# Two-layer hybrid encoder on one core: value blocks by half, keys by part over all partitions, and a new spread of gate pieces

## What is computed

```
h    = RMSNorm(x)
proj = h @ w_in[l]                      # q, k, v and gate columns of three mixers
ya   = windowed attention A  (+-128 tokens, sink, bias)
yb   = dense attention B     (rotary positions)
yc   = dilated attention C   (three patterns: (128,1), (512,4), (2048,16), merged by their denominators)
x    = x + concat[ya*silu(gA), yb*silu(gB), yc*silu(gC)] @ w_out[l]
```

## Time and profile before

| | |
|---|---|
| median of three runs | 2765.29 us |
| the profiled execution | 2772.11 us, of which the span is 2769.8 us |
| TensorE busy | 2732.1 us, 99% of the span |
| VectorE, ScalarE, GpSimd busy | 58%, 43%, 28% |
| mean granted TensorE clock | 0.994 of full |
| layer 0: quads, unit 4, unit 5 | 651.04 to 706.29, to 755.70, to 806.98 us |
| layer 1: quads, unit 4 | 2021.79 to 2082.67, to 2133.26 us |

### The profile page before, as it was taken

One profiled execution on the slowest core, in us unless ns is written; L12 is line 12 of the kernel. 1 busy time (PEld: TensorE's weight loads), 2 busy tenths in 40 slices (PEclk: granted clock), 3 DMA queues, 4 the chain that ended last, 5 costly groups with the idle time before them and its releaser, 6 DMA issues. The chain is left out here.

```text
span 2769.8 us, 43315 instructions
## 1 busy us (share of the span) xinstructions
PE 2732.1 (99%) x14505; PEld 2447.6 (88%) x14505; DVE 1609.7 (58%) x3865; ACT 1184.4 (43%) x2813; POOL 763.8 (28%) x882
## 2 busy tenths in 40 slices
PE   8999999999999999999999999999999999999999
PEld 7888899988999999988888888999889999999887
DVE  3345644434676677677743465444346767776776
ACT  4322222224565566544542222222246655665443
POOL 0333333320343344300003334333203433443000
PEclk9999999999999999999999999999999999999999
DMA  5356566668544542464524565656774445325535
GB/s 175 106 183 200 180 185 188 181 179 233 142 132 123 128 112 82 177 219 130 197 85 142 176 195 173 200 170 188 191 218 134 117 118 149 101 69 217 192 122 182
DMA packets 436214, 442.52 MB, mean 160 GB/s; under 512 B 97591, under 2 KB 327127, under 8 KB 435996
## 3 DMA queue, kind: packets, MB, share of 16 engines
q1 hardware_dynamic: 435996, 439.77, 53.3%
HBM read 313.91 MB, written 125.75 MB: 159 GB/s over the span
## 5 line engine op out<-in xcount | busy, mean ns | idle before, releaser
L1834 ACT CAST w_hi<-w_raw 128x512 fp32r<-128x512 f32 x640 | 397.0, 622 | 697.8 <-PE bank L1605 430.6
L1603 PE MATMUL bank<-w_hi,act_hi 128*128 128x512 f32 x1728 | 689.2, 399 | 0.0
L2120 DVE TENSOR_TENSOR w_lo<-w_raw,w_hi 128x512 fp32r<-128x512 f32 x640 | 460.1, 722 | 384.9 <-ACT w_hi L1834 383.3
L1605 PE MATMUL bank<-w_hi,act_lo 128*128 128x512 f32 x1728 | 679.0, 393 | 0.0
L1604 PE MATMUL bank<-w_lo,act_hi 128*128 128x512 f32 x1728 | 677.6, 392 | 0.0
L1605 PEld LDWEIGHTS bank<-w_hi,act_lo 128*128 128x128 f32 x1728 | 372.6, 216 | 54.1
L1603 PEld LDWEIGHTS bank<-w_hi,act_hi 128*128 128x128 f32 x1728 | 373.3, 216 | 50.1
L1604 PEld LDWEIGHTS bank<-w_lo,act_hi 128*128 128x128 f32 x1728 | 373.3, 216 | 48.7
L1659 PE MATMUL bank<-act_hi,w_hi 128*128 128x384 f32 x1024 | 349.2, 341 | 0.0
L1661 PE MATMUL bank<-act_hi,w_lo 128*128 128x384 f32 x1024 | 346.3, 338 | 0.0
L1660 PE MATMUL bank<-act_lo,w_hi 128*128 128x384 f32 x1024 | 345.7, 338 | 0.0
(11 more groups left out here) (136 smaller groups left out, 4406.5 us busy)
## 6 DMA issues: line engine op xcount, KB each, us to landing
w_raw<-w_in SPq DMA_DIRECT2D x144, 512.0 KB, 4.8
w_sums<-sum_out SPq DMA_DIRECT2D x32, 1280.0 KB, 6.7
w_raw<-w_sums SPq DMA_DIRECT2D x80, 512.0 KB, 4.0
sum_in<-w_out SPq DMA_DIRECT2D x64, 512.0 KB, 5.6
heads_t<-turned SPq DMA_DIRECT2D x240, 128.0 KB, 2.4
q_t<-heads_t SPq DMA_DIRECT2D x192, 128.0 KB, 2.1
k_t<-keys_t SPq DMA_DIRECT2D x48, 384.0 KB, 5.8
w_raw<-w_out SPq DMA_DIRECT2D x32, 512.0 KB, 3.7
```

The source lines that it names most:

```text
L1603: pe.matmul(acc[t][:], hi, w_hi[:, W_AT[n]:W_AT[n] + SLAB], start=(k == 0), stop=False)
L1605: last = pe.matmul(acc[t][:], lo, w_hi[:, W_AT[n]:W_AT[n] + SLAB], start=False, stop=(k == KC - 1))
L1834: nc.scalar.copy(w_hi[:, W_AT[n]:W_AT[n] + SLAB], w_raw[:, load % W_RAW, j, :]).then_inc(w_hi_done, 1)
L2120: nc.vector.tensor_tensor(w_lo[:, W_AT[n]:W_AT[n] + SLAB], w_raw[:, load % W_RAW, j, :], w_hi[:, W_AT[n]:W_AT[n] + SLAB].bitcast(F32), ALU ...
```

## The change

Three edits, and nothing that is computed changes.

1. `load_blocks` takes the half as an argument. The blocks of unit 3 are loaded by half: tiles 0 to 2 at items 17 to 20 (they wait for the value products of unit 1's first three steps alone), tiles 3 to 5 at items 20 to 23. Each half has its own semaphore, and a value product waits for its own half.
2. `load_keys` makes its two DMAs by part: each writes one part (high or low) to all 128 partitions, reading 64 rows of 3072 bytes twice. The bytes are the same.
3. `piece_schedule` has new costs: open quads 3 (were 1), packed quads 4 (were 3), steps of unit 4 6 (were 8), all others 8. By the table that this gives, turns 0 to 23 have 25 pieces (were 14), unit 4 has 44 (was 58), units 5, 8 and 11 have one more each. The splits of gate chunks 4 to 7 move from turns 9, 15, 22 and 25 to 5, 9, 12 and 16; the drain of the first tile's second half from turn 25 to 16, that of the second tile's first half from 32 to 28; the fifth gate load on SP (512 KB) from item 20 to 14, the sixth from 29 to 21.

```
--- before.py
+++ after.py
@@ -565,7 +565,8 @@
 
 def piece_schedule():
 
-    cost = [3 if packed(st["unit"]) else {"Q": 1}.get(st["kind"], 8) for st in STEPS]
+    first_pairs = min(st["u"] for st in STEPS if st["kind"] != "Q")
+    cost = [4 if packed(st["unit"]) else 3 if st["kind"] == "Q" else 6 if st["u"] == first_pairs else 8 for st in STEPS]
     done, now, between = [], 0, PIECES - PIECES_FIRST - PIECES_LAST
     for i in range(N_LOOP):
         if i < N_STEPS:
@@ -634,8 +635,8 @@
 PARTS_AT = at_items((i, x["step"] + MIX_LAG) for i, x in enumerate(ITEMS) if x["kind"] == "Q")
 KEYS_AT = at_items((u, UNIT_LAST[u - KV_SLOTS] + 1) for u in range(KV_SLOTS, len(ATT_UNITS)))
 VALUES_IN_AT = at_items((u, UNIT_LAST[u - KV_SLOTS] + PAIR_LAG + 1) for u in range(KV_SLOTS, len(ATT_UNITS)) if not packed(ATT_UNITS[u]))
-BLOCKS_AT = at_items(((u, c), UNIT_LAST[u - KV_SLOTS] + PAIR_LAG + c)
-                     for u, x in enumerate(ATT_UNITS) if packed(x) and u >= KV_SLOTS for c in range(CLASSES))
+BLOCKS_AT = at_items(((u, half, c), UNIT_START[u - KV_SLOTS] + (half + 1) * (TT // 2) - 1 + PAIR_LAG + c)
+                     for u, x in enumerate(ATT_UNITS) if packed(x) and u >= KV_SLOTS for half in range(2) for c in range(CLASSES))
 MERGE_IN_AT = at_items((mc, end - 2 * TT + 1 + PAIR_LAG + 1 if mc == 0 else MERGE_END[mc - 1] + OWN_TURN + 2) for mc, end in enumerate(MERGE_END))
 BIASES_AT = at_items(((b, heads), BIAS_LAST[b - 2] + 1 + (1 + heads[0] if BIAS_SETS[b][1] is None else 0))
                      for b in range(2, len(BIAS_SETS)) for heads in (((0,), (1,), (2,), (3,)) if BIAS_SETS[b][1] is None else ((0, 1),)))
@@ -904,7 +905,7 @@
         packed_chain = sem("packed_chain")
         blocks_cleared = sem("blocks_cleared")
         ones_set = sem("ones_set")
-        blocks_loaded = sem("blocks_loaded")
+        blocks_loaded = [sem(f"blocks_loaded{i}") for i in range(2)]
         merge_mins = sem("merge_mins")
         merge_args = sem("merge_args")
         merge_exps = sem("merge_exps")
@@ -1241,8 +1242,9 @@
                     sp.wait_ge(scored, l * N_STEPS + UNIT_LAST[u - KV_SLOTS] + 1)
                 elif l > 0:
                     sp.wait_ge(scored, l * N_STEPS)
-                for to in range(2):
-                    sp.dma_start(k_t[to * DH:(to + 1) * DH, :, slot, :, :].bitcast(F32), keys_t[unit["k"]])                        .then_inc(k_loaded[slot], 16)
+                for part in range(2):
+                    rows = bass.AP(keys_t.tensor, (unit["k"] * DH * 2 + part) * TOKENS, [[0, 2], [2 * TOKENS, DH], [1, TOKENS]])
+                    sp.dma_start(k_t[:, part, slot, :, :].rearrange("p t c -> p (t c)").bitcast(F32), rows).then_inc(k_loaded[slot], 16)
 
             def load_values(l, u):
 
@@ -1266,16 +1268,15 @@
                                  v_rows[rows, unit["v"] * DH:(unit["v"] + 1) * DH].rearrange("(t p) n -> p t n", p=P))\
                         .then_inc(shifted_loaded[unit["j"]], 16)
 
-            def load_blocks(l, u, c):
+            def load_blocks(l, u, half, c):
 
                 unit = ATT_UNITS[u]
                 sp.wait_ge(ones_set, 2 * CLASSES * (l + 1))
                 if u >= KV_SLOTS:
-                    sp.wait_ge(pv_done, l * N_STEPS + UNIT_LAST[u - KV_SLOTS] + 1)
+                    sp.wait_ge(pv_done, l * N_STEPS + UNIT_START[u - KV_SLOTS] + (half + 1) * (TT // 2))
                 sp.wait_ge(v_stored, 16 * (l * V_STORES + V_BEFORE_LAST))
                 rows = v_rows[:, unit["v"] * DH:(unit["v"] + 1) * DH].rearrange("(h t m c) n -> h c m t n", h=2, t=TT // 2, c=CLASSES)
-                for half in range(2):
-                    sp.dma_start(blocks[half][c * PACK:(c + 1) * PACK, :, c, 0:DH], rows[half, c]).then_inc(blocks_loaded, 16)
+                sp.dma_start(blocks[half][c * PACK:(c + 1) * PACK, :, c, 0:DH], rows[half, c]).then_inc(blocks_loaded[half], 16)
 
             def load_bias(l, b, heads=range(4)):
                 u, hp = BIAS_SETS[b]
@@ -1470,8 +1471,8 @@
                         load_values(l, 0)
                     if slot == KEYS_SLOT + 1:
                         load_keys(l, 1)
-                        for c in range(CLASSES):
-                            load_blocks(l, 1, c)
+                        for half, c in itertools.product(range(2), range(CLASSES)):
+                            load_blocks(l, 1, half, c)
 
                 for t in range(TT):
                     store_values(l, NS_IN - 1, t)
@@ -1484,8 +1485,8 @@
                         load_keys(l, u)
                     for u in VALUES_IN_AT.get(it, ()):
                         load_values(l, u)
-                    for u, c in BLOCKS_AT.get(it, ()):
-                        load_blocks(l, u, c)
+                    for u, half, c in BLOCKS_AT.get(it, ()):
+                        load_blocks(l, u, half, c)
                     for b, heads in BIASES_AT.get(it, ()):
                         load_bias(l, b, heads)
                     for mc in MERGE_IN_AT.get(it, ()):
@@ -1726,8 +1727,8 @@
                         quad_taken(pe, l, q - 2)
                 pe.wait_ge(ones_set, 2 * CLASSES * (l + 1))
                 if packed(st["unit"]):
-                    pe.wait_ge(blocks_loaded, 16 * 2 * CLASSES * (l * KV_C + st["unit"]["j"] + 1))
                     half, at = divmod(st["t"], TT // 2)
+                    pe.wait_ge(blocks_loaded[half], 16 * CLASSES * (l * KV_C + st["unit"]["j"] + 1))
                     pe.matmul(o[:, 0:CLASSES * (DH + 1)], prob_t[:, n % PT_SLOTS, 0:P],
                               blocks[half][:, at, :, :].rearrange("p c d -> p (c d)"), start=True, stop=True).then_inc(pv_done, 1)
                     return
```

2 lines of the change are left out of this document (1 added, 1 removed).

## The result

| | before | changed |
|---|---|---|
| median | 2765.0 us | 2919.8 us (2919.4 to 2923.5) |
| ratio | 1 | 1.0559 (1.0544 to 1.0574) |
| span of the profiled execution | 2769.8 us | 2917.3 us |

The forecast was 2747 us, its range 2738 to 2758. The time lies far outside. The profile after is read in the same order as that of before.

The account below looks back on a forecast made before the run. TensorE, busy for 99% of the span, was taken as the bound. Gains 4.2 + 9.6 (quads) + 2.9 + 4.1 (unit 4) - 1.6 (returned pieces) = 19.2 us off 2765.3 gave 2746.1; with 1 us off for clock, 2747, range 2738 to 2758.

Parts of the forecast that it names:

- The keys over all partitions: Key loads into 128 partitions: about 2 us less in the queue per unit, bounds nothing and 2.2, taken 1.7.
- The rival with the other sign: Units 4 of both layers: many small waits bring TensorE to half clock; slower, 2810 us if all their work; chance 0.03.
- Unit 4 at 46.5 us: First unit of pairs, fourteen pieces fewer: 49.4 to 46.5 us, gain 2.9 us, and 4.1 in layer 1.
- The loop: Unit 4: ScalarE and VectorE wait for one another, not for TensorE; 41.6 us for twenty turns stay.
- Unit 4 does not shorten: Rival: the loop in unit 4 starts no earlier; 7 us less gain, 2754 us; chance 0.1.
- The pieces in the quads: Eleven pieces more add 5.7 us a layer and cover early gaps; quads 51.0 and 51.3 us, 0.5 left over.
- nothing that can be told: Rival: loads and stores land as late as before, pieces only lengthen the quads; about zero, 2765 us; chance 0.05.
- The blocks by half: Quads: unit 3's first-half value blocks land before TensorE needs them, removing waits of 4.35 and 5.0 us.
- I take the whole gap: Quads: TensorE's whole wait for the value blocks counted as gain, 4.35 and 5.0 us.
- The queue is the next wait: Rival: keys no faster or SP held at item 21; 8 us in all with half clock, 2755 us; chance 0.17.
- The clock loss: Mostly quads: half-clock loss of 3.3 and 9.2 us; 1 us off the gain as part may miss the median.
- The clock loss is not in the median: Rival: the median lacks the profiled execution's half-clock loss; 11 us of the sum go, 2757 us; chance 0.12.

Follow-up runs that it names:

- The runs with 128, 8 and 2: Kernel before, its key DMAs reading 128 rows of 3 KB as one list, cut 8 x 16, or 2 x 64: 2760.7, 2777.1 and 2918.8 us.
- experiment two: Changed kernel with the keys loaded as before, blocks by half and moved pieces kept: 2772.9 us, ratio 1.0028.
- experiments two and four: Two: changed kernel with the keys loaded as before, 2772.9 us; four: kernel before with the value blocks by half alone, 2761.6 us.

## Why the prediction was wrong

- **The keys over all partitions: this step failed, and it alone decided.** It had bounds of nothing and 2.2 us a pair and took 1.7 as gain. The lower end excluded a loss, though the same sentence noted that the reading side was new ("reads each row twice in another order"), and no row of before showed a DMA of that form. The pair takes 18.8 us instead of 7.4. Its size for sixteen engines was right as a landing time: 1.6 us with 128 rows in a list. In the kernel's time that was worth 1 to 4 us, at or under what can be told. What I compared, 384 KB into 64 partitions with 384 KB into 128, was the writing side; what decided was the reading side, a list whose slowest dimension is two.
- What I cited of the Trainium skill ("SBUF — State Buffer", the DMA port swizzle) speaks for the edit; what it says in "DMA: Bandwidth & Descriptors" (section "Why a DMA increments its semaphore by 16 and not by 1") speaks against it, and I didn't weigh it. The number it asks for stood in the changed line itself: a first dimension of two. The runs with 128, 8 and 2 agree with it (16, 8 and 2 updates after the issue); that 64 partitions reach half of the ports no run here tests by itself.
- **The rival with the other sign** was the clock of unit 4. It put the loss in the wrong place and at 0.03. A rival "the new DMA is slower than the old" was not among them; the range of 2738 to 2758 followed from that.
- **Unit 4 at 46.5 us: wrong as well**, 48.9 and 48.4 in experiment two. The loop was read rightly, but it started later than forecast: step 26's minima start 5.8 us after unit 4 does in layer 0, where the forecast comes to 4.1. The first turn took 3.05 us at half clock (a piece's matmuls stand 0.32 us apart instead of 0.17; the granted clock is 0.51 from 706 to 711 us), and two turns of two pieces take 3.7 us even at full clock (1.92 and 1.83 in the kernel before), not 3.3. From there twenty turns took 42.5 us, not 41.6. And I stopped at step 48. The loop goes on through unit 5, which I left at 51.3 and which took 53.6: units 4 and 5 together take 102.5 and 102.0 us against 100.7 and 101.9. Of 7.0 us of forecast gain nothing came. The rival "Unit 4 does not shorten" (0.1) had the size, for another reason.
- **The pieces in the quads: added work right, cover wrong.** 5.7 us a layer were added, and TensorE's busy time rose by 4.2 us in layer 0 with the clock better by 0.05. The quads were forecast with 0.5 us of idle time and have 6.4 and 4.0. With no gain in unit 4 behind them the pieces are the loss: 9.9 us alone, 11.3 between experiments two and four. My rival of "nothing that can be told" had this mechanism and priced it at zero.
- **The blocks by half: the gap did go, in all kernels with this edit.** "I take the whole gap" failed: waits at the quads' queries and for VectorE took 3.7 of the 9.3 us back. The rival "The queue is the next wait" named the place; with 0.17 it was too low, and moving the keys one item back didn't help.
- **The clock loss.** This term was mis-sized: I took 1 us off for it. The record has 107 more executions of the kernel before, each with its mean granted clock. The 22 at 0.998 have a median of 2762.3 us, the 8 at 0.993 one of 2772.3, and the median clock is 0.997. The profiled execution, at 0.994 and with 60.9 us in the quads of layer 1, took 2772.1 us, so most of the 7 us by which it exceeds the median goes with its clock, and the median execution doesn't have them to give back. The rival "The clock loss is not in the median" (0.12) was nearer. The run with the blocks alone shows it: its profiled span is 11 us shorter than before's, its median 3 us.

Of the 155 us, then, some 147 are the keys' (2919.8 less 2772.9), some 10 to 11 the pieces', and the blocks give 3 back, which by itself can't be told from nothing. These are differences taken in one order; alone on the kernel before, the keys' edit costs 159.

## What to carry to other kernels

Before a DMA's list is rewritten, write down the slowest dimension of both sides for the old and the new form: with two in the source a pair of loads took 18.8 us, with 128 it took 5.8, and the loads queued behind it were late too. A quick sign in the trace is the number of semaphore updates of a DMA. A term whose form no row shows needs a bound on the side of loss. A profiled execution above the median may hold clock loss that no change can win back in the median. Where an engine is busy for 100% of a stretch, look whether two others wait for one another in every turn before work is taken from it, and follow their loop past the end of the stretch.

## What was not expected of the hardware

- Such a pair of loads holds others up in two ways. The next load, 1.9 us behind it, landed 18.0 us after its issue, as late as the keys themselves; and its issue on SP took 5.93 us where the row of before shows 1.19. Why SP was held, and on what the load waited, wasn't tried.
- Stores of 64 KB take 0.65 us each of SP's time to issue (10.33 us for sixteen): with 24 instead of 12 ahead of the quads' first load, the quads began with gaps of 5.1 and 4.1 us. How much of that is the issue and how much the added bytes wasn't tried.
